# Feed-forward layers of a three-layer transformer block: split inputs tile by tile before the norm is known, apply the norm factor to the up projections' outputs

## The chip, the core and the metric

The kernel runs on one core of a Trainium2 chip. Its time is the device time of one execution in microseconds (us). Engines are called by these names: TensorE (PE, matrix products), VectorE (DVE), ScalarE (ACT), GpSimd (POOL), SyncE (SP, here only issuing loads).

## What is computed

Three layers over a sequence of 512 tokens of width 1024 in float32: a windowed-attention layer, a recurrent (RWKV) layer, and a layer that mixes three attentions. Each ends in a feed-forward part, and these three parts are what the change touches:

```
def rms_norm(x, g):
    y = xf * lax.rsqrt(jnp.mean(xf * xf, axis=-1, keepdims=True) + NORM_EPS)
    return (y * g.astype(F32)).astype(x.dtype)
...
        x = x + y
        x = x + conv_ffn(rms_norm(x, norm_ch[i]), ffn_w_up[i], ffn_conv_w[i], ffn_conv_b[i], ffn_w_down[i])
...
    u = h @ w_up                      # 1024 -> 5632
    acc = up[:, :s] * conv_w[0] + conv_b
    for t in range(1, CONV_WIDTH):    # three taps along the sequence
        acc = acc + up[:, t:t + s] * conv_w[t]
    gate, val = jnp.split(acc, 2, axis=-1)
    return (jax.nn.silu(gate) * val) @ w_down      # 2816 -> 1024
```

The third layer's feed-forward part has no convolution: silu(h @ w_gate) * (h @ w_up), then @ w_down. The factor rsqrt(mean(x*x)) is one number for each token, so it can be multiplied in before a product with weights or after it.

## The kernel before

**Layout.** Activations lie transposed: 128 features on the partitions, 512 tokens along the row. A matrix [128, 512] of this kind is one activation tile; x (`xT`) is 8 of them (`KT` = 8). A product with a weight matrix runs over output tiles (`tile()` on TensorE). The list `tile_table()` gives their order through the program: `swa_o` (8 tiles), `up0` (44), `down0` (8), the recurrent layer, `rw_o` (8), `up1` (44), `down1` (8), the third layer's attentions, `out` (8), `up2` (44), `down2` (8). An `up` tile sums over 8 input tiles kt, a `down` tile over 22.

**Split operands.** Each float32 operand is split into a high part and a low part (x minus high), and each kt costs three matmuls of 512 columns: high*high, low*high, high*low (lines 1503 to 1505), so an `up` tile is 24 matmuls. Weights come by SyncE into a ring of 5 pieces of up to 8 kt; ScalarE makes the high part (`split_high`, line 289), GpSimd the low part (`split_low`, line 298). The piece for the tile three ahead is split when a tile ends (`advance(t)`). Activations are split by ScalarE (`act_split`, line 499) and VectorE (`dve_split`, line 505); `wait_split` lets TensorE wait for the low part of one kt. `HS` holds the split inputs of the next product. In a float32 product that isn't split (the norm's sum, line 1585; the head sums, line 1538) one matmul instruction shows as two records.

**Output tiles** go to two PSUM banks in turn (`bank_of(t)`). Tile t may start when tile t-2's bank has been read for the last time; `release[t]` names the semaphore. For `swa_o`, `rw_o` and `out` it is the addition to x (`add_x`, line 2243 on VectorE).

**The norm ahead of a feed-forward part** (`ch0`, `ch1`, `ffn`). While the product before it streams, ScalarE squares each x tile after it was added (`square`, line 1850) and GpSimd sums the squares (line 2102). When the last one is in, TensorE multiplies by ones (`norm`, line 1585, into bank 7), ScalarE forms the factor by Ln and Exp (lines 1857 and 1858) in `M.nrs`, and VectorE multiplies x by gain and factor, tile by tile (line 2187), into `F.stmp`, from which the split is made. Only then can the first `up` tile's matmuls run, kt by kt.

**The up phase.** In layers 0 and 1 ScalarE reads the finished bank (line 1969: middle tap and bias, into `F.acc`), VectorE adds the outer taps from the same bank (lines 2372 and 2374), ScalarE takes Silu (line 1977), VectorE multiplies gate and value (line 2379) and the product is split into `F.hid`. In layer 2 ScalarE takes Silu from the bank (line 1988), and VectorE multiplies the other bank into it (line 2384). All engines run their own list of instructions in order; semaphores set the rest.

Of the kernel before, what the change touches and what calls it, by code (L numbers as in the profile page):

```python
# [15 lines left out]
P = 128  # L16
# [133 lines left out]
def build(nc, ctx, x_in, mem_in, w_in, vec_in, row_in, const_in, small_in, x_spill, out):  # L150
# [192 lines left out]
    M.score = at(o, NBUF, 512); o += NBUF * 512  # L343
    M.pts = at(o, 2, 512); o += 1024
# [5 lines left out]
    M.q = at(o, KT, T); o += KT * T  # L350
    M.k = at(o, 4, T); o += 4 * T
    M.v = at(o, TT, 256); o += TT * 256
    M.turned = at(o, 4, 512); o += 4 * 512
    kp_swa = at(o, CONST_SIZE[1]); o += CONST_SIZE[1]
# [6 lines left out]
    F.stmp = at(o, 2, 512); o += 1024  # L361
    assert o <= NORM, o
# [166 lines left out]
    o += 2 * KT * T  # L529
    R.r = at(o, KT, T); o += KT * T  # L530
# [44 lines left out]
    R.z = pair(CORE, 4, T) + pair(TMP, 2, T) + pair(TMP + 6 * 512, 2, T)  # L575
# [913 lines left out]
    def _(pe):  # L1489
# [21 lines left out]
        def fm(name, rhs, gate=None):  # L1511
            for k, t in enumerate(tiles_of[name]):
                tile(t, rhs, gate if k == 0 else None)
# [233 lines left out]
        fm("swa_o", h_split, gate=lambda kt: wait_split(pe, "swa_o", kt))  # L1747
        norm("ch0")
# [9 lines left out]
        norm("ch1")  # L1758
# [34 lines left out]
        norm("ffn")  # L1793
# [4 lines left out]
    def _(act):  # L1798
# [53 lines left out]
        def norm(name, width=T, dst=None, tmp=None, first=False):  # L1852
# [3 lines left out]
            r = M.nrs[:, 0:width]  # L1856
# [50 lines left out]
        def attend_swa():  # L1907
            for s in range(len(PAIRS) + 6):
# [21 lines left out]
                if 0 <= r < len(PAIRS) and r % TT == TT - 1:  # L1930
                    act.wait_ge(SW_O, r + 1)
                    act_split(act, "swa_o", r // TT, lambda p: OT_BANKS[r // TT % 2], HS[r // TT])
# [26 lines left out]
        def ffn(L):  # L1959
            if L < 2:  # L1960
                for n, t in enumerate(tiles_of[f"up{L}"]):
                    i, g = n // 2, n % 2
                    c = 44 * L + n
                    advance(t)
                    wait_tile(act, t)
# [620 lines left out]
```

## Time and profile before

| | us |
|---|---|
| median of 3 runs (3051.27 to 3064.58) | 3053.04 |
| the profiled execution | 3059.92 |
| its span in the trace | 3058.1 |

TensorE's granted clock is 0.976 of full speed on average. Durations below come from the profiled execution, whose span is 1.8 us shorter than its time. Rows of the timeline give start, busy time, engine, line, operation, output and inputs; in square brackets stands the time that the engine was idle before the row and what ended it. Rows that follow each other closely on one line are merged (x2). A row of groups gives count, busy us and mean ns. A matmul row overlaps the next: matmuls start 0.23 us apart at full clock although a row says 0.39.

### The profile page before, as it was taken

What the parts mean: (1) busy time and instruction counts of PE and PEld (TensorE: products, weight loads), DVE (VectorE), ACT (ScalarE), POOL (GpSimd) and SP (SyncE); (2) the same over time, 40 slices, a digit from 0 to 9 for tenths busy, and PEclk for the clock granted to TensorE, in tenths of its full rate; (3) what the DMA queues carried; (4) which work ended last, traced back from release to release, by engine and by line L of the source; (5) the groups of instructions that cost most, each with busy time, mean ns of one, the idle gap of its engine ahead of it and who ended that gap; (6) DMA issues with size and microseconds to landing.
All of it is one profiled execution on the core that took longest, in us unless ns stands there. A gap on an engine that the chain in (4) does not pass through costs nothing.

```text
span 3058.1 us, 55232 instructions
## 1 busy us (share of the span) xinstructions
PE 2852.6 (93%) x23558; PEld 2232.2 (73%) x23558; DVE 1122.0 (37%) x2425; ACT 1241.6 (41%) x2288; POOL 1153.5 (38%) x659
## 2 busy tenths in 40 slices
PE   6998999969999999988999989899999989999999
PEld 4666888847677777776888866477777777778887
DVE  3473333045656677653333111602211224321110
ACT  4473443223455555543443223534443444332221
POOL 3204444553443222213444444043333342534443
PEclk9999999979999999998999999899999999999999
DMA  3202332222210000011232222032211231323322
GB/s 135 62 8 76 96 97 92 94 77 81 86 45 7 7 7 7 5 36 56 90 97 94 92 89 66 4 122 74 80 62 65 72 101 47 107 76 97 96 89 78
DMA packets 59364, 211.96 MB, mean 69 GB/s; under 512 B 6833, under 2 KB 7089, under 8 KB 58737
## 3 DMA queue, kind: packets, MB, share of 16 engines
q1 hardware_dynamic: 56160, 192.96, 19.9%
q0 software_dynamic: 2384, 14.06, 1.3%
q8 instruction: 187, 3.06, 0.4%
q10 hardware_dynamic: 576, 1.41, 0.1%
q14 instruction: 57, 0.46, 0.1%
HBM read 204.21 MB, written 4.19 MB: 68 GB/s over the span
## 4 chain that ended last, share of the span: by engine, by line
PE 82%; DVE 9%; ACT 5%; issue 2%; POOL 1%; DMA 0%; POOLq 0%; SPq 0%; ACTq 0%; DVEq 0%
PE banks L1503 20%; PE banks L1505 20%; PE banks L1504 20%; PE banks L723 7%; DVE low L505 2%; PE banks L1624 2%; PE banks L1538 2%; PE banks L1602 1%; PE banks L638 1%; DVE arena L2187 1%; DVE arena L2215 1%; ACT arena L1827 1%; ACT arena L1826 1%; PE banks L774 1%; PE banks L716 1%
## 5 line engine op out<-in xcount | busy, mean ns | idle before, releaser
L298 POOL TENSOR_TENSOR low<-arena,high 128x1024 fp32r<-128x1024 f32 (+1 forms) x378 | 871.8, 2307 | 1408.0 <-ACT high L289 1407.9
L1503 PE MATMUL banks<-high,high 128*128 128x512 f32 (+1 forms) x2864 | 1168.5, 408 | 83.7 <-DVE low L505 65.2
L1504 PE MATMUL banks<-low,high 128*128 128x512 f32 (+1 forms) x2864 | 1131.7, 395 | 0.0
L1505 PE MATMUL banks<-high,low 128*128 128x512 f32 (+1 forms) x2864 | 1131.2, 395 | 0.0
L289 ACT ACTIVATE high<-arena 128x1024 fp32r<-128x1024 f32 (+1 forms) x378 | 383.8, 1016 | 938.3 <-PE banks L1505 931.5
L1503 PEld LDWEIGHTS banks<-high,high 128*128 128x128 f32 x2864 | 544.7, 190 | 263.6 <-issue 53.9
L1504 PEld LDWEIGHTS banks<-low,high 128*128 128x128 f32 x2864 | 546.0, 191 | 128.8 <-issue 12.3
L1505 PEld LDWEIGHTS banks<-high,low 128*128 128x128 f32 x2864 | 545.1, 190 | 125.4
L723 PE MATMUL banks<-arena 64*64 64x64 f32 x7680 | 291.5, 222 | 28.0 <-ACT arena L1018 12.2
L723 PEld LDWEIGHTS banks<-arena 64*64 64x64 f32 x7680 | 251.0, 135 | 86.9 <-ACT arena L1018 31.5
L1018 ACT ACTIVATE arena<-banks 128x256 f32<-128x256 f32 (+2 forms) x384 | 144.7, 384 | 173.5 <-PE banks L723 163.6
L2243 DVE TENSOR_TENSOR arena<-banks,arena 128x512 f32<-128x512 f32 x48 | 33.1, 692 | 449.8 <-PE banks L1505 442.7
L505 DVE TENSOR_TENSOR low<-arena,high 128x512 fp32r<-128x512 f32 (+1 forms) x182 | 166.2, 914 | 28.8 <-ACT high L499 27.5
L2372 DVE SCALAR_TENSOR_TENSOR arena<-banks,arena 128x511 f32<-128x511 f32 x88 | 66.0, 750 | 294.5 <-ACT arena L1969 294.5
L2215 DVE SCALAR_TENSOR_TENSOR arena<-banks,arena 128x512 f32<-128x512 f32 (+1 forms) x56 | 41.0, 732 | 328.1 <-ACT arena L1827 328.1
L499 ACT ACTIVATE high<-arena 128x512 fp32r<-128x512 f32 (+1 forms) x182 | 111.6, 615 | 95.3 <-DVE arena L1209 52.4
L1167 POOL TENSOR_TENSOR arena<-arena 128x128 f32<-128x128 f32 x64 | 27.7, 453 | 306.0 <-DVE arena L1426 305.9
L1400 DVE TENSOR_TENSOR arena<-banks,arena 128x128 f32<-128x128 f32 x320 | 88.3, 289 | 146.7 <-PE banks L723 144.5
L1826 ACT ACTIVATE arena<-banks,arena 128x512 f32<-128x512 f32 (+1 forms) x56 | 37.6, 672 | 163.2 <-PE banks L1538 163.2
L2384 DVE TENSOR_TENSOR arena<-banks,arena 128x512 f32<-128x512 f32 x22 | 15.2, 692 | 214.4 <-PE banks L1505 214.4
L1840 ACT ACTIVATE arena<-banks 128x512 f32<-128x512 f32 (+2 forms) x50 | 28.9, 579 | 145.6 <-PE banks L1505 145.5
L2374 DVE SCALAR_TENSOR_TENSOR arena<-banks,arena 128x511 f32<-128x511 f32 x88 | 66.0, 750 | 3.1
(222 smaller groups left out, 2711.5 us busy)
## 6 DMA issues: line engine op xcount, KB each, us to landing
arena<-weights SPq DMA_DIRECT2D x306, 512.0 KB, 3.5
arena<-weights SPq DMA_DIRECT2D x48, 448.0 KB, 3.2
arena<-weights SPq DMA_DIRECT2D x24, 256.0 KB, 2.6
arena<-tables POOLq DMA_DIRECT2D x13, 448.0 KB, 4.6
arena<-x_t SPq DMA_DIRECT2D x4, 512.0 KB, 7.3
x_spill<-arena POOLq DMA_DIRECT2D x1, 2048.0 KB, 9.1
arena<-small_weights POOLq DMA_DIRECT2D x16, 128.0 KB, 2.6
arena<-x_spill POOLq DMA_DIRECT2D x1, 2048.0 KB, 9.1
```

Source lines behind the costliest of these rows:

```text
L289: act.activation(wsplit[w % SPLITS][0][:, 0:n], ring[w % RING][:, 0:n], ACT.Copy).then_inc(w_high, 1)
L298: pool.tensor_tensor(lo[:, 0:n], ring[w % RING][:, 0:n], hi[:, 0:n].bitcast(F32), ALU.subtract).then_inc(w_low, 1)
L499: act.activation(dst[0], src((s0 + i) % 2), ACT.Copy).then_inc(act_high, 1)
L505: dve.tensor_tensor(dst[1], src((s0 + i) % 2), dst[0].bitcast(F32), ALU.subtract).then_inc(act_low, 1)
L723: mm = pe.matmul(bank[hf(p), col + C * q:col + C * q + C], lhs(hf(p), q), rhs(hf(p), q), start=True, stop=True)
L1018: a2.inc(act.activation(dst, PJ[h][:, 0:n], ACT.Copy), f"{name}_{h}")
L1400: d2.inc(dve.tensor_tensor(u, PI[h][:, 0:P], u, ALU.add), f"U{s}_{h}")
L1503: pe.matmul(dst, hi[:, c], x[0], start=kt == 0, stop=False)
L1504: pe.matmul(dst, hi[:, c], x[1], start=False, stop=False)
L1505: mm = pe.matmul(dst, lo[:, c], x[0], start=False, stop=kt == kts_of[t] - 1)
L1826: link(act.activation(r, psum[2 + H % 2][:, 0:width], ACT.Ln, bias=EPS, scale=1.0 / group))
L2215: dve.scalar_tensor_tensor(o_, bank[:, 0:width], gain, s.rs[:, H % 2, 0:width], ALU.mult, ALU.mult) \
```

## The change

The three norms before feed-forward parts (`ch0`, `ch1`, `ffn`) are no longer applied to x. `add_x` on VectorE multiplies each x tile by the gain alone as soon as it is added, into `F.stmp`, and both halves of the split are made while the product before is still streaming. TensorE runs the norm's sum as `mid` of the first `up` tile, behind its kt 4. The factor goes to a buffer of its own, `F.rs`. VectorE multiplies every `up` output tile by it into `F.up` (two buffers), which releases the bank (`up_scaled`); the middle tap, the outer taps, Silu and the gate's product read `F.up`, in SBUF, where they read PSUM before. VectorE's outer taps of tile n-1 now stand behind the scaling of tile n.

Since `HS` is now written while the product before is read, two inputs moved: the window attention's outputs are split into `M.o` instead of `HS`, with the layer's buffers laid out anew, and the recurrent layer's split outputs `R.z` lie in other places.

```diff
@@
+    M.o = pair(o, KT, T)
...
+    F.up = at(o, 2, 512); o += 1024
+    F.rs = at(o, 512); o += 512
...
-    for L in range(2):
+    up_scaled = sem("up_scaled")
+    for L in range(3):
         for n, t in enumerate(tiles_of[f"up{L}"]):
-            release[t] = (conv_done, 44 * L + n + 1)
-    for n, t in enumerate(tiles_of["up2"]):
-        release[t] = (hid_ready, 2 * FT + n // 2 + 1) if n % 2 else (glu_gate, n // 2 + 1)
+            release[t] = (up_scaled, 44 * L + n + 1)
...
-    R.z = pair(CORE, 4, T) + pair(TMP, 2, T) + pair(TMP + 6 * 512, 2, T)
+    R.z = [[nc.alloc_sbuf_tensor_at(f"z_{part}{j}", [P, T], F32R, offset=start + 4 * (a + j * T))[:, :]
+            for part, a in (("high", CORE), ("low", RAT))] for j in range(KT)]
@@ TensorE
         def ffn(L):
             name = ("ch0", "ch1", "ffn")[L]
-            fm(f"up{L}", h_split, gate=lambda kt: wait_split(pe, name, kt))
+            fm(f"up{L}", h_split, gate=lambda kt: wait_split(pe, name, kt), mid=lambda: norm(name))
...
-        norm("ch0")
         ffn(0)
@@ ScalarE
+            def square_and_split(j):
+                square(norm_name, j, xT)
+                if norm_name in ("ch0", "ch1", "ffn"):
+                    act_split(act, norm_name, j, lambda p: F.stmp[:, p, :], HS[j])
+
             for j, t in enumerate(tiles_of[name]):
                 if j and norm_name:
-                    square(norm_name, j - 1, xT)
+                    square_and_split(j - 1)
                 for p in pieces_of[t]:
                     if norm_name and p == pieces_of[tiles_of[name][-1]][-1]:
-                        square(norm_name, KT - 1, xT)
+                        square_and_split(KT - 1)
                     split_high(act, p + SPLITS)
...
         def ffn(L):
+            norm(("ch0", "ch1", "ffn")[L], to=F.rs)
+            for n, t in enumerate(tiles_of[f"up{L}"]):
+                i, g = n // 2, n % 2
+                c, m = 44 * L + n, FT * L + i
+                advance(t)
+                if L < 2:
+                    act.wait_ge(up_scaled, c + 1)
                     if c >= 4:
                         act.wait_ge(hid_ready, FT * L + i - 1)
                     col = L * 132 + 44 + g * FT + i
-                    act.activation(F.acc[:, c % 4, :], bank_of(t)[:, :], ACT.Identity,
+                    act.activation(F.acc[:, c % 4, :], F.up[:, n % 2, :], ACT.Identity,
...
-        norm("ch0", dst=HS, tmp=F.stmp)
         ffn(0)
@@ VectorE
-        def add_x(name):
+        def add_x(name, scaled=None):
+
+            def low(k):
+                dve_split(dve, scaled, k, lambda p: F.stmp[:, p, :], HS[k])
             for k, t in enumerate(tiles_of[name]):
                 wait_tile(dve, t)
                 dve.tensor_tensor(xT[:, k, :], bank_of(t)[:, :], xT[:, k, :], ALU.add).then_inc(x_ready, 1)
+                if scaled:
+                    g, o_ = NGAIN[scaled]
+                    dve.wait_ge(x_ready, XBASE[name] + k + 1)
+                    dve_free(dve, scaled, k)
+                    dve.tensor_scalar(F.stmp[:, (SG[scaled][0] + k) % 2, :], xT[:, k, :], vcol(g, o_ + k), None, ALU.mult) \
+                       .then_inc(N_H, 1)
+                    if k:
+                        low(k - 1)
+            if scaled:
+                low(KT - 1)
...
+            def taps(n):
+                g, i, c = n % 2, n // 2, 44 * L + n
+                a, b = F.acc[:, c % 4, :], F.up[:, g, :]
+                dve.wait_ge(sem("conv_mid"), c + 1)
+                link(dve.scalar_tensor_tensor(a[:, 1:T], b[:, 0:T - 1], vcol("conv_w", L * 132 + g * FT + i),
+                                              a[:, 1:T], ALU.mult, ALU.add))
+                dve.scalar_tensor_tensor(a[:, 0:T - 1], b[:, 1:T], vcol("conv_w", L * 132 + 88 + g * FT + i),
+                                         a[:, 0:T - 1], ALU.mult, ALU.add).then_inc(conv_done, 1)
...
+            dve.wait_ge(N_RS, NORMS.index(("ch0", "ch1", "ffn")[L]) + 1)
+            for n, t in enumerate(tiles):
+                wait_tile(dve, t)
+                if n >= 2 and L < 2:
+                    dve.wait_ge(conv_done, 44 * L + n - 1)
+                elif n >= 2:
+                    dve.wait_ge(*((hid_ready, 2 * FT + n // 2) if n % 2 else (glu_gate, n // 2)))
+                dve.tensor_tensor(F.up[:, n % 2, :], bank_of(t), F.rs, ALU.mult).then_inc(up_scaled, 1)
+                if L < 2:
+                    if n:
+                        taps(n - 1)
+                    if n >= 2 and n % 2 == 0:
+                        product(n // 2 - 1)
+                elif n % 2:
+                    product(n // 2)
...
-        add_x("swa_o")
-        norm("ch0", dst=HS, tmp=F.stmp)
+        add_x("swa_o", "ch0")
         ffn(0)
```

How the instruction lists move, by their order in the program. **VectorE, end of `swa_o` and start of `up0`.** Before, the eight additions stand together, then gain and factor (L2187) alternate with the low parts (L505) of `HS`:

```order
L2243 TENSOR_TENSOR arena<-banks,arena 128x512 x8
L2187 SCALAR_TENSOR_TENSOR arena<-arena 128x512 x2
L505 TENSOR_TENSOR low_57<-arena,high_56 128x512
L2187 SCALAR_TENSOR_TENSOR arena<-arena 128x512
L505 TENSOR_TENSOR low_59<-arena,high_58 128x512
```

Now the end of the same list reads (L2244 is the addition, L2249 the gain alone, L508 a low part, L2406 the scaling of an `up` output tile, L2380 and L2382 its outer taps):

```order
L2244 TENSOR_TENSOR arena<-banks,arena 128x512
L2249 TENSOR_SCALAR arena<-arena 128x512
L508 TENSOR_TENSOR low_69<-arena,high_68 128x512
L508 TENSOR_TENSOR low_71<-arena,high_70 128x512
L2406 TENSOR_TENSOR arena<-banks,arena 128x512 x2
L2380 SCALAR_TENSOR_TENSOR arena<-arena 128x511
L2382 SCALAR_TENSOR_TENSOR arena<-arena 128x511
```

All but the last addition's gain and low parts now stand between additions; behind the last one there are one gain and two low parts, where sixteen instructions stood.

**VectorE, one pair of tiles within `up0`.** Before (L2379 is the product of gate and value):

```order
L2372 SCALAR_TENSOR_TENSOR arena<-banks,arena 128x511
L2374 SCALAR_TENSOR_TENSOR arena<-banks,arena 128x511
L2372 SCALAR_TENSOR_TENSOR arena<-banks,arena 128x511
L2374 SCALAR_TENSOR_TENSOR arena<-banks,arena 128x511
L2379 TENSOR_TENSOR arena<-arena 128x512
L505 TENSOR_TENSOR low_75<-arena,high_74 128x512
```

Now (L2395 is the product):

```order
L2406 TENSOR_TENSOR arena<-banks,arena 128x512
L2380 SCALAR_TENSOR_TENSOR arena<-arena 128x511
L2382 SCALAR_TENSOR_TENSOR arena<-arena 128x511
L2406 TENSOR_TENSOR arena<-banks,arena 128x512
L2380 SCALAR_TENSOR_TENSOR arena<-arena 128x511
L2382 SCALAR_TENSOR_TENSOR arena<-arena 128x511
L2395 TENSOR_TENSOR arena<-arena 128x512
L508 TENSOR_TENSOR low_91<-arena,high_90 128x512
```

Two instructions with one input in PSUM are added to a pair, and the four taps lose their PSUM input: both their inputs are now in SBUF.

**TensorE, from `swa_o`'s last matmuls into `up0`.** Before, the norm's sum (L1585) stands between the two products:

```order
L1503 MATMUL banks<-high_70,high_50 128x512
L1504 MATMUL banks<-low_71,high_50 128x512
L1505 MATMUL banks<-high_70,low_51 128x512
L1585 MATMUL banks<-arena 128x512
L1503 MATMUL banks<-high_56,high_52 128x512
```

Now it (L1590) stands behind 15 of `up0`'s first 24 matmuls (kt 4 ends there, kt 5 follows):

```order
L1508 MATMUL banks<-high_64,high_52 128x512
L1509 MATMUL banks<-low_65,high_52 128x512
L1510 MATMUL banks<-high_64,low_53 128x512
L1590 MATMUL banks<-arena 128x512
L1508 MATMUL banks<-high_66,high_52 128x512
```

## Rows read from the trace of the kernel before

**Rows 1.** The page: busy us (share of the span) and instructions of each engine.
```profile
PE 2852.6 (93%) x23558; PEld 2232.2 (73%) x23558; DVE 1122.0 (37%) x2425; ACT 1241.6 (41%) x2288; POOL 1153.5 (38%) x659
```

**Rows 2.** Stretches: length, busy us (instructions) by engine, clock, DMA share, GB/s.
```profile
270.00:279.00 9.00, 7.73 (x25) 4.53 (x24) 7.57 (x12) 3.36 (x7) 0.00 (x0) 0.85 0.00 0
300.00:400.00 100.00, 100.00 (x432) 81.05 (x431) 38.95 (x54) 40.43 (x54) 43.37 (x18) 1.00 0.30 95
...
1436.00:1450.00 14.00, 9.15 (x20) 4.59 (x20) 10.14 (x15) 6.31 (x10) 2.54 (x2) 0.63 0.12 39
```

**Rows 3.** VectorE's timeline at the norm ahead of `up0`.
```profile
261.19 0.69 DVE L2243 TENSOR_TENSOR arena<-banks,arena 128x512 f32<-128x512 f32 x1 [4.89 <-PE banks L1505]
266.58 0.75 DVE L2187 SCALAR_TENSOR_TENSOR arena<-arena 128x512 f32<-128x512 f32 x1 [4.70 <-ACT arena L1858]
```

**Rows 4.** TensorE's timeline at the same place.
```profile
263.94 1.13 PE L1585 MATMUL banks<-arena 128*128 128x512 f32 x2 [2.79 <-POOL arena L2102]
268.87 0.77 PE L1503 MATMUL banks<-high,high 128*128 128x512 f32 x1 [3.80 <-DVE low L505]
...
274.33 0.51 PE L1503 MATMUL banks<-high,high 128*128 128x512 f32 x1 [0.42 <-DVE low L505]
...
275.72 0.50 PE L1503 MATMUL banks<-high,high 128*128 128x512 f32 x1 [0.42 <-DVE low L505]
```

**Rows 5.** ScalarE's timeline: the ends of `up0`'s first and second tile.
```profile
278.96 1.06 ACT L289 ACTIVATE high<-arena 128x1024 fp32r<-128x1024 f32 x1 [1.85 <-PE banks L1505]
...
284.54 1.06 ACT L289 ACTIVATE high<-arena 128x1024 fp32r<-128x1024 f32 x1 [3.85 <-PE banks L1505]
```

**Rows 6.** VectorE and ScalarE around the norm ahead of `up1`.
```profile
1433.55 0.69 DVE L2243 TENSOR_TENSOR arena<-banks,arena 128x512 f32<-128x512 f32 x1 [4.89 <-PE banks L1505]
1451.99 1.06 ACT L289 ACTIVATE high<-arena 128x1024 fp32r<-128x1024 f32 x1 [1.85 <-PE banks L1505]
```

**Rows 7.** The same two around the norm ahead of `up2`.
```profile
2674.78 0.69 DVE L2243 TENSOR_TENSOR arena<-banks,arena 128x512 f32<-128x512 f32 x1 [4.87 <-PE banks L1505]
2692.53 1.06 ACT L289 ACTIVATE high<-arena 128x1024 fp32r<-128x1024 f32 x1 [1.84 <-PE banks L1505]
```

**Rows 8.** TensorE: an unsplit 128x512 product between split matmuls, clock up.
```profile
42.16 0.40 PE L1505 MATMUL banks<-high,low 128*128 128x512 f32 x1
42.40 1.02 PE L1538 MATMUL banks<-arena 128*128 128x512 f32 x2
...
43.48 0.39 PE L1504 MATMUL banks<-low,high 128*128 128x512 f32 x1
```

**Rows 9.** ScalarE's last square, GpSimd's last sum, and Exp ahead of `up0`.
```profile
261.92 0.63 ACT L1850 ACTIVATE arena<-arena 128x512 f32<-128x512 f32 x1 [4.67 <-DVE arena L2243]
...
262.62 1.27 POOL L2102 TENSOR_TENSOR arena<-arena 128x512 f32<-128x512 f32 x1 [2.17 <-ACT arena L1850]
...
265.83 0.72 ACT L1858 ACTIVATE arena<-arena 128x512 f32<-128x512 f32 x1
```

**Rows 10.** VectorE, one line in the window attention: ns min/median/max, forms.
```profile
L2318 DVE TENSOR_SCALAR arena<-arena x64: 345/382/423, 139.5 to 213.0; 128x256 f32<-128x256 f32 x32, 128x384 f32<-128x384 f32 x32
```

**Rows 11.** Groups by line in 280 to 520 (`up0`): busy us, mean ns, idle before.
```profile
L2372 DVE SCALAR_TENSOR_TENSOR arena<-banks,arena 128x511 f32<-128x511 f32 x43 | 32.2, 750 | 143.3 <-ACT arena L1969 143.3
L2379 DVE TENSOR_TENSOR arena<-arena 128x512 f32<-128x512 f32 x21 | 16.1, 766 | 1.2 <-ACT arena L1977 0.5
L505 DVE TENSOR_TENSOR low<-arena,high 128x512 fp32r<-128x512 f32 x20 | 13.6, 679 | 0.0
L298 POOL TENSOR_TENSOR low<-arena,high 128x1024 fp32r<-128x1024 f32 x42 | 101.2, 2409 | 143.8 <-ACT high L289 143.8
```

**Rows 12.** GpSimd and VectorE at the end of `mix2`; then the latter's line, ns min/median/max.
```profile
2630.96 2.49 POOL L298 TENSOR_TENSOR low<-arena,high 128x1024 fp32r<-128x1024 f32 x1 [0.40 <-ACT high L289]
2631.21 3.39 DVE L505 TENSOR_TENSOR low<-arena,high 128x512 fp32r<-128x512 f32 x2
L505 DVE TENSOR_TENSOR low<-arena,high x2: 678/1734/2789, 2631.2 to 2633.9; 128x512 fp32r<-128x512 f32 x2
```

More of the change, by code:

```diff
@@ L529, in build @@
     o += 2 * KT * T
+    RAT = o
     R.r = at(o, KT, T); o += KT * T
@@ L1746, in _ @@
         attend_swa()
-        fm("swa_o", h_split, gate=lambda kt: wait_split(pe, "swa_o", kt))
-        norm("ch0")
+        fm("swa_o", lambda kt: M.o[kt], gate=lambda kt: wait_split(pe, "swa_o", kt))
         ffn(0)
@@ L1850, in square, with norm @@
             act.activation(M.nsq[:, i % 2, 0:width], src[:, j, :], ACT.Square).then_inc(N_SQ, 1)
-        def norm(name, width=T, dst=None, tmp=None, first=False):
+        def norm(name, width=T, dst=None, tmp=None, first=False, to=M.nrs):
             n = NORMS.index(name)
             act.wait_ge(N_ST, n + 1)
-            r = M.nrs[:, 0:width]
+            r = to[:, 0:width]
             link(act.activation(r, psum[7][:, 0:width], ACT.Ln, bias=EPS, scale=1.0 / D))
@@ L1977, in ffn @@
                         act.activation(F.sg[:, m % 2, :], F.acc[:, (44 * L + 2 * i) % 4, :], ACT.Silu).then_inc(sem("silu"), 1)
[L1978 to L1990 removed]
+                elif g == 0:
+                    act.wait_ge(up_scaled, c + 1)
+                    if i >= 2:
+                        act.wait_ge(hid_ready, m - 1)
+                    act.activation(F.sg[:, i % 2, :], F.up[:, 0, :], ACT.Silu).then_inc(glu_gate, 1)
+                if g and i:
+                    act_split(act, f"hid{L}", i - 1, lambda p: F.stmp[:, p, :], F.hid[i - 1])
             act_split(act, f"hid{L}", FT - 1, lambda p: F.stmp[:, p, :], F.hid[FT - 1])
@@ L2016, in _ @@
         stream_tiles("rw_o", "ch1")
-        norm("ch1", dst=HS, tmp=F.stmp)
         ffn(1)
@@ L2081, in _ @@
         stream_tiles("out", "ffn")
-        norm("ffn", dst=HS, tmp=F.stmp)
         ffn(2)
@@ L2363, in ffn @@
             tiles = tiles_of[f"up{L}"]
-            for i in range(FT):
-                tmp = F.stmp[:, (SG[f"hid{L}"][0] + i) % 2, :]
+            def taps(n):
[6 more added lines that the diff above has]
+                                         a[:, 0:T - 1], ALU.mult, ALU.add).then_inc(conv_done, 1)
@@ L2366, in ffn, with product @@
+            def product(i):
                 dve_free(dve, f"hid{L}", i)
                 if L < 2:
-                    for g in range(2):
-                        n = 44 * L + 2 * i + g
-                        a, b = F.acc[:, n % 4, :], bank_of(tiles[2 * i + g])
-                        dve.wait_ge(sem("conv_mid"), n + 1)
-                        link(dve.scalar_tensor_tensor(a[:, 1:T], b[:, 0:T - 1], vcol("conv_w", L * 132 + g * FT + i),
-                                                      a[:, 1:T], ALU.mult, ALU.add))
-                        dve.scalar_tensor_tensor(a[:, 0:T - 1], b[:, 1:T], vcol("conv_w", L * 132 + 88 + g * FT + i),
-                                                 a[:, 0:T - 1], ALU.mult, ALU.add).then_inc(conv_done, 1)
@@ L2388, in ffn @@
+            if L < 2:
+                taps(2 * FT - 1)
+                product(FT - 1)
             low(FT - 1)
@@ L2415, in _ @@
         dve.wait_ge(x_back, 16)
-        add_x("rw_o")
-        norm("ch1", dst=HS, tmp=F.stmp)
+        add_x("rw_o", "ch1")
         ffn(1)
@@ L2473, in _ @@
         mix(2)
-        add_x("out")
-        norm("ffn", dst=HS, tmp=F.stmp)
+        add_x("out", "ffn")
         ffn(2)
```

53 lines of the change are left out of this document (15 added, 38 removed).

## Prediction

> **What bounds the kernel now.** I read the page's busy times first. TensorE is busy for 2852.6 of 3058.1 us, 93%, and no other engine for more than 41% [rows 1], so only time in which TensorE stands still or runs slowly can be won. The table of stretches shows where it does neither: from 300 to 400, inside `up0`, it is busy for all 100.00 us at clock 1.00 [rows 2]. An `up` tile there takes 284.54 - 278.96 = 5.58 us from end to end [rows 5], 0.2325 us a matmul. The timelines then show the place that the change is about. VectorE begins the last addition of `swa_o` at 261.19, right at that tile's end; the first matmul of `up0` starts at 268.87 [rows 3, 4], and the first tile's end shows as the weight split that ScalarE starts at 278.96 [rows 5]. The reader is to see two losses in these 17.77 us: the wait for sum, factor and first split, and then a tile that is fed with one kt every 275.72 - 274.33 = 1.39 us [rows 4], where three matmuls take 0.70. The clock is low on top: 0.85 from 270 to 279, and 0.63 from 1436 to 1450 at the second norm [rows 2]. The same distance is 1451.99 - 1433.55 = 18.44 us ahead of `up1` [rows 6] and 2692.53 - 2674.78 = 17.75 us ahead of `up2` [rows 7].
>
> **What the change takes from these distances.** If TensorE goes straight on, the distance from the last addition's start to the first `up` tile's end is one tile, 5.58 us; both marks start within hundredths of a us behind a tile's end, which I neglect. To this comes the norm's sum, which now stands in the tile. Its price in the flow is in [rows 8]: from the matmul at 42.16 to the one at 43.48 there are 1.32 us with one split matmul and one unsplit product between them; without the latter it would be two steps of 0.23, so it costs 0.86. After the change the distance is 5.58 + 0.86 = 6.44 us, and the gains are 17.77 - 6.44 = 11.33, 18.44 - 6.44 = 12.00 and 17.75 - 6.44 = 11.31. The sum is 34.6 us.
>
> **Is everything there in time?** Let E be the end of the last tile of `swa_o`. Its addition takes 0.69 [rows 3], to E+0.75. The gain alone on 128x512 has no row; the same operation on 256 and 384 columns takes 0.345 to 0.423 [rows 10], and a 512-column instruction with two SBUF inputs 0.75 [rows 3], so it lies between 0.4 and 0.75 and I take 0.5, nearer to the row of its own form. Low parts of kt 0 to 5 were made between earlier additions, where VectorE sat idle for 4.89 us at each tile [rows 3]. Low part of kt 6 ends near E+2.0. For kt 7 ScalarE must square first (0.63 from 261.92, about E+0.8 [rows 9]), then make the high part at about E+1.5 to 2.1; GpSimd's last sum, 1.27 [rows 9], may come ahead of the low part, which then ends near E+4.1. TensorE reaches kt 6 at E+4.2 + 0.86 and kt 7 at E+4.9 + 0.86. Both are in time, kt 7 with 1.6 us to spare. The norm's sum comes behind 15 matmuls, E+3.5. Before, it started at 263.94 [rows 4], 2.8 us behind an E of 261.1; if GpSimd is held up by one low part (0.68) it is E+3.5, so a wait of 0 to 0.5 is possible here. I take none. The factor was ready when Exp ended, 265.83 + 0.72 - 263.94 = 2.6 us behind the sum's start [rows 4, 9]; that gives E+6.1, and the first `up` tile ends at E+6.44, so VectorE can scale it at once.
>
> **Costs in the up phase.** VectorE gets one 128x512 multiplication per `up` tile, 132 in all. The nearest row is the addition of the same shape with one PSUM input, 0.69 us [rows 3]. For a pair of tiles of `up0` VectorE had four taps of 0.75, one product of 0.77 and one low part of 0.68 [rows 11], 4.45 us of 2 x 5.58 = 11.16; now it has 4.45 + 1.38 = 5.83. The bank of tile n is free at about 0.8 us behind its end, while tile n+2 starts one tile, 5.58 us, later. Price: nothing, hidden by TensorE's own 5.58. ScalarE waits for the scaling before its middle tap; behind that wait in its list are Silu, one high part and the next tile's weight split. That piece is wanted by TensorE only two tiles, 11.16 us, after the tile's end that starts it, and split plus GpSimd's low part take 1.06 + 2.41 = 3.5 [rows 5, 11]. At the end of `up0` the last hidden tile is now late by about a scaling, a pair of taps and a GpSimd instruction, at most 0.7 + 1.5 + 2.4 more; it is wanted by the first `down` tile behind 21 kt, 21 x 0.70 = 14.6 us. Nothing there either. The added multiplications and gains are thus free as long as VectorE keeps up. `M.o` and `R.z` only move data; they cost nothing where neither adds an instruction. The window attention's and recurrent layer's last splits keep their place in the lists.
>
> **What speaks against it: VectorE and GpSimd get in each other's way.** [rows 12] show a low part, two SBUF inputs, that began at 2631.21 beside a GpSimd split begun at 2630.96 for 2.49 us: it lasted 2.789 instead of 0.678 and ended at 2634.0, which is GpSimd's end, 2633.45, and most of a low part. The taps with a PSUM input ran at 0.750 on average next to 2.41 us of GpSimd work in every tile [rows 11]. The change turns these four taps of a pair into instructions with two SBUF inputs. So add what excludes each other: 4 x 0.75 + 0.77 + 0.68 + 2 x 2.41 = 9.27 us of 11.16 for a pair, and with the two scalings, if none overlaps GpSimd, 10.65. It still fits, by 0.5 us in the strictest count and 1.9 in the other; lateness doesn't pile up, since a scaling that comes late runs beside GpSimd. I take nothing, with 0 to 1 us a pair as bounds.
>
> The Trainium skill says the same as a rule (page "SBUF — State Buffer", section "SBUF: two separate sides"): a VectorE instruction with two SBUF inputs and a GpSimd instruction hold the shared ports exclusively, and the other one waits for the whole instruction. [rows 12] agree, 2.789 against 0.678 us. The rule is what rival C rests on. By it as by the row the sum stays at 34.6 us, since 10.65 is under 11.16; without either, VectorE alone would need 5.83.
>
> **The rivals.**
> A, the forecast: TensorE goes straight on at all three places, -34.6 us. Chance 0.72.
> B, gaps remain: the sum or the last split comes late by the port exclusion or by GpSimd's queue (its last sum stands behind the sum before it), 1 to 3 us at each of three norms, or the factor delays the first banks. Gain 34.6 - 3 to 34.6 - 9, that is 25.6 to 31.6 us. For it speaks the 0 to 0.5 us that I found as slack for the sum; against it that each late item has two tiles' cover. Chance 0.18.
> C, the other side: exclusion on the shared ports makes VectorE the bound of `up0` and `up1`. It decides when what excludes each other and the scalings take more than 11.16 us a pair; each further us costs 44 us over 44 pairs, so the kernel is slower than before from 11.16 + 34.6 / 44 = 11.95 us on, against my 10.65. At 12.2 us it would be 1.04 x 44 - 34.6 = +11 us. Chance 0.04.
> D, the gain isn't there: the 11 us come back elsewhere, say as low clock later or a late weight ring, and the time stays within 10 us. Against it: the stretch from 300 to 400 shows clock 1.00 under full load [rows 2]. Chance 0.06.
>
> **The numbers.** The profiled execution took 3059.92 us, 6.9 above the median of the runs, 3053.04. By the profile the change gives 3059.92 - 34.6 = 3025.3; a gain in waits doesn't depend on which run it is taken from, so for the median I predict 3053.04 - 34.6 = 3018.4 us. The runs of before spread from 3051 to 3065, so a median can be off by some 5 us either way. The range reaches from 3018.4 - 9 = 3009.4 (the spread of runs, and a few us that a rounded duration may hide) to 3053 - 22 = 3031, which takes in case B with some spread. About 0.5% (15 us) is what a measurement of this kernel can tell from no change. Faster by more than that, under 3037.8, are A, B and a little of D: 0.91. Within it: most of D and an edge of C, 0.06. Slower: 0.03.
>
> **What the next profile would show.** Right: between the last addition of `swa_o`, `rw_o` or `out` and the first weight split of the `up` phase 6.4 us instead of 17.8 to 18.4; no TensorE row with an idle time over 0.5 us there; clock 1.00 throughout; tiles of `up0` still 5.58 us apart; VectorE's taps longer than 0.75 on average, because one in a tile waits for GpSimd. Wrong would be: `up` tiles over 5.6 us apart (C), a TensorE wait at the norm's sum or at kt 6 and 7 (B), a stretch of low clock or of waits that before wasn't there (D). The time before the last `swa_o` tile and the `down` phases should be the same to within 1 us.

## The result and the profile after

The changed kernel takes 3024.27 us (median of 4 runs, 3016.72 to 3026.67) beside 3053.37 us for the kernel before (4 runs). The ratio is 0.9893 with an interval of 0.9863 to 0.9924, which is 32.7 us less, with 23 to 42 us as bounds; the ratio is estimated from all the runs, while the two medians alone differ by 29.1 us, inside these bounds. Run again beside 17 runs of the kernel before (`changed_again` below) the ratio is 0.9893 again, now with 0.9879 to 0.9908. The forecast was 34.6 us less, and 3018.4 us.

The page of the changed kernel, in the form of [rows 1]:

```profile
span 3024.9 us, 55470 instructions
...
PE 2841.6 (94%) x23558; PEld 2230.9 (74%) x23558; DVE 1415.7 (47%) x2557; ACT 1248.3 (41%) x2288; POOL 1170.0 (39%) x659
```

The span fell from 3058.1 to 3024.9, by 33.2 us. TensorE runs the same 23558 instructions. VectorE has 132 instructions more, one for each `up` tile, and 293.7 us more of busy time, far more than 132 x 0.69 = 91 us. The rest is not work; below it turns out to be mostly waiting.

VectorE's timeline at the end of `swa_o`, which answers to [rows 3]:

```profile
260.64 0.69 DVE L2244 TENSOR_TENSOR arena<-banks,arena 128x512 f32<-128x512 f32 x1 [3.76 <-PE banks L1510]
261.37 0.49 DVE L2249 TENSOR_SCALAR arena<-arena 128x512 f32<-128x512 f32 x1
261.77 2.39 DVE L508 TENSOR_TENSOR low<-arena,high 128x512 fp32r<-128x512 f32 x2
267.15 0.69 DVE L2406 TENSOR_TENSOR arena<-banks,arena 128x512 f32<-128x512 f32 x1 [2.98 <-PE banks L1510]
```

ScalarE's, which answers to [rows 5, 9]:

```profile
261.37 0.64 ACT L1852 ACTIVATE arena<-arena 128x512 f32<-128x512 f32 x1 [4.14 <-DVE arena L2244]
261.91 0.61 ACT L502 ACTIVATE high<-arena 128x512 fp32r<-128x512 f32 x1
...
265.71 0.72 ACT L1860 ACTIVATE arena<-arena 128x512 f32<-128x512 f32 x1
267.14 1.06 ACT L289 ACTIVATE high<-arena 128x1024 fp32r<-128x1024 f32 x1 [0.70 <-PE banks L1510]
...
272.71 1.06 ACT L289 ACTIVATE high<-arena 128x1024 fp32r<-128x1024 f32 x1 [3.81 <-PE banks L1510]
```

TensorE's, which answers to [rows 4, 8]:

```profile
263.70 0.40 PE L1510 MATMUL banks<-high,low 128*128 128x512 f32 x1
263.93 1.02 PE L1590 MATMUL banks<-arena 128*128 128x512 f32 x2
264.39 0.80 PE L1508 MATMUL banks<-high,high 128*128 128x512 f32 x1
265.02 0.39 PE L1509 MATMUL banks<-low,high 128*128 128x512 f32 x1
```

From the last addition (260.64) to the first `up` tile's end (267.14) there are now 6.50 us where there were 17.77. No TensorE row there has an idle time in square brackets, and the sum lies in the flow: from the start of the matmul at 263.70 to the start of the one at 265.02 there are 1.32 us, which is two steps of 0.23 for the matmuls at 263.70 and 264.39 and 0.86 for the sum between them. Low parts end at 264.16, the factor at 266.43, and VectorE scales the first bank at once, at 267.15. The other two places, VectorE's last addition and then ScalarE's split at the first tile's end:

```profile
1423.83 0.69 DVE L2244 TENSOR_TENSOR arena<-banks,arena 128x512 f32<-128x512 f32 x1 [3.79 <-PE banks L1510]
1430.33 1.06 ACT L289 ACTIVATE high<-arena 128x1024 fp32r<-128x1024 f32 x1 [0.70 <-PE banks L1510]
2652.80 0.69 DVE L2244 TENSOR_TENSOR arena<-banks,arena 128x512 f32<-128x512 f32 x1 [3.76 <-PE banks L1510]
2659.29 1.06 ACT L289 ACTIVATE high<-arena 128x1024 fp32r<-128x1024 f32 x1 [0.70 <-PE banks L1510]
```

The distances are 6.50 and 6.49 us, where [rows 6] gave 18.44 and [rows 7] 17.75. The three gains are 11.27 + 11.94 + 11.26 = 34.47 us. Stretches around the places and in the up phases, with the columns of [rows 2]:

```profile
225.00:275.00 50.00, 50.00 (x215) 40.21 (x214) 17.06 (x26) 20.17 (x28) 33.41 (x18) 1.00 0.30 95
270.00:390.00 120.00, 120.00 (x518) 97.30 (x517) 97.22 (x83) 50.70 (x65) 51.94 (x22) 1.00 0.29 95
1390.00:1430.00 40.00, 40.00 (x170) 31.92 (x171) 19.29 (x23) 17.52 (x26) 32.31 (x16) 1.00 0.29 93
1430.00:1660.00 230.00, 230.00 (x992) 186.46 (x991) 192.08 (x162) 97.24 (x124) 99.01 (x41) 1.00 0.30 96
```

TensorE is busy all the time at clock 1.00, also in the stretch that answers to 1436 to 1450 before, where the clock was 0.63. At the third place, from 2650 to 2690, the clock is 1.00 too. In `up0`, groups of VectorE from 270 to 510 (against [rows 11]):

```profile
L2382 DVE SCALAR_TENSOR_TENSOR arena<-arena 128x511 f32<-128x511 f32 x43 | 114.8, 2670 | 1.5
L2380 DVE SCALAR_TENSOR_TENSOR arena<-arena 128x511 f32<-128x511 f32 x43 | 31.9, 742 | 0.0
L2406 DVE TENSOR_TENSOR arena<-banks,arena 128x512 f32<-128x512 f32 x43 | 29.7, 692 | 38.0 <-PE banks L1510 37.5
```

One tap in a tile takes 2670 ns instead of 750, the other 742 (the forecast had said that one in a tile would wait for GpSimd). The timeline of one tile says why, VectorE first, then GpSimd:

```profile
401.53 0.74 DVE L2380 SCALAR_TENSOR_TENSOR arena<-arena 128x511 f32<-128x511 f32 x1
402.31 2.77 DVE L2382 SCALAR_TENSOR_TENSOR arena<-arena 128x511 f32<-128x511 f32 x1
405.17 0.69 DVE L2395 TENSOR_TENSOR arena<-arena 128x512 f32<-128x512 f32 x1
```

```profile
402.12 2.41 POOL L298 TENSOR_TENSOR low<-arena,high 128x1024 fp32r<-128x1024 f32 x1 [3.15 <-ACT high L289]
```

GpSimd's split began at 402.12 and ended at 404.53. The tap that came 0.19 us later ended at 405.08, 0.55 behind it, which is most of its own 0.75. Over 88 tiles with taps this comes to 88 x 1.92 = 169 us, the larger part of the 293.7.

The Trainium skill (page "SBUF — State Buffer", section "SBUF: two separate sides") has the rule that the later of the two waits for the whole instruction of the earlier. The trace agrees: the tap begun beside GpSimd's split took 2.77 us where the one before it took 0.74.

### The profile page after: what moved, and what is told of

The parts are those of the page before. It is cut to its first block, busy times and chain, and to the rows that moved or that the text cites. A ratio compares the mean times of both kernels' runs of the same rounds, so it can differ in the third digit from the quotient of the medians.

```text
span 3024.9 us, 55470 instructions
## 1 busy us (share of the span) xinstructions
PE 2841.6 (94%) x23558; PEld 2230.9 (74%) x23558; DVE 1415.7 (47%) x2557; ACT 1248.3 (41%) x2288; POOL 1170.0 (39%) x659
## 4 chain that ended last, share of the span: by engine, by line
PE 83%; DVE 8%; ACT 5%; issue 2%; POOL 1%; DMA 1%; POOLq 0%; SPq 0%; ACTq 0%; DVEq 0%
PE banks L1508 21%; PE banks L1509 20%; PE banks L1510 20%; PE banks L728 7%; PE banks L1629 2%; PE banks L1543 2%; DVE low L508 2%; PE banks L1607 1%; PE banks L643 1%; DVE arena L2213 1%; ACT arena L1829 1%; ACT arena L1828 1%; PE banks L779 1%; PE banks L721 1%; DVE arena L1214 1%
## 5 line engine op out<-in xcount | busy, mean ns | idle before, releaser
L298 POOL TENSOR_TENSOR low<-arena,high 128x1024 fp32r<-128x1024 f32 (+1 forms) x378 | 886.9, 2347 | 1358.2 <-ACT high L289 1358.1
L1508 PE MATMUL banks<-high,high 128*128 128x512 f32 (+1 forms) x2816 | 1145.5, 407 | 69.3 <-DVE low L508 50.9
L1509 PE MATMUL banks<-low,high 128*128 128x512 f32 (+1 forms) x2816 | 1110.1, 394 | 0.0
L1510 PE MATMUL banks<-high,low 128*128 128x512 f32 (+1 forms) x2816 | 1110.0, 394 | 0.0
L1509 PEld LDWEIGHTS banks<-low,high 128*128 128x128 f32 x2816 | 535.3, 190 | 127.9 <-issue 13.0
L1510 PEld LDWEIGHTS banks<-high,low 128*128 128x128 f32 x2816 | 534.4, 190 | 122.9
L2382 DVE SCALAR_TENSOR_TENSOR arena<-arena 128x511 f32<-128x511 f32 x88 | 235.2, 2672 | 3.1
L2244 DVE TENSOR_TENSOR arena<-banks,arena 128x512 f32<-128x512 f32 x48 | 33.2, 691 | 419.5 <-PE banks L1510 411.1
L508 DVE TENSOR_TENSOR low<-arena,high 128x512 fp32r<-128x512 f32 (+1 forms) x174 | 205.8, 1184 | 26.9 <-ACT high L502 25.6
L2406 DVE TENSOR_TENSOR arena<-banks,arena 128x512 f32<-128x512 f32 x132 | 91.3, 692 | 219.6 <-PE banks L1510 218.4
L2232 DVE COPY arena<-banks 128x512 f32<-128x512 f32 (+1 forms) x30 | 19.7, 656 | 109.7 <-PE banks L1563 109.7
```

What stands on the lines that cost most here:

```text
L298: pool.tensor_tensor(lo[:, 0:n], ring[w % RING][:, 0:n], hi[:, 0:n].bitcast(F32), ALU.subtract).then_inc(w_low, 1)
L508: dve.tensor_tensor(dst[1], src((s0 + i) % 2), dst[0].bitcast(F32), ALU.subtract).then_inc(act_low, 1)
L1508: pe.matmul(dst, hi[:, c], x[0], start=kt == 0, stop=False)
L1509: pe.matmul(dst, hi[:, c], x[1], start=False, stop=False)
L1510: mm = pe.matmul(dst, lo[:, c], x[0], start=False, stop=kt == kts_of[t] - 1)
L2382: dve.scalar_tensor_tensor(a[:, 0:T - 1], b[:, 1:T], vcol("conv_w", L * 132 + 88 + g * FT + i), a[:, 0:T - 1], ALU.mult, ALU.add).then_inc ...
```

## The experiments

Ratios are to the kernel before in the same job (medians 3059.09, 3058.49 and 3058.13 us). Distance is the time from the last addition's start to the first `up` tile's end; 6.50 in the changed kernel.

**1. The moved buffers alone.** `layout_only` is the kernel before with the new buffers `M.o` and `R.z`.

```diff
+    M.o = pair(o, KT, T)
...
+    R.z = [[nc.alloc_sbuf_tensor_at(...
...
-            fm("swa_o", h_split, ...
+            fm("swa_o", lambda kt: M.o[kt], ...
```

> Kernel before, with only the two moves of buffers (the window attention's outputs into M.o, R.z in its new places). Theory (buffers are free, the gain is the three norm gaps): same time as before, within 3 us, the three distances from last addition to first up tile's end still 17.8, 18.4 and 17.8 us. Rival (the moved buffers cost the 2 us that the recurrent part was longer in the changed kernel's profile): about 2 us slower, with the low clock at the end of the recurrent part always 16 instead of 10.5 us long.

Measured: 3057.64 us, ratio 1.0000 (0.9989 to 1.0011). The move costs nothing that can be measured, and nothing of the gain is in it.

**2. Layers apart.** `third_only` changes layer 2 alone, `first_two` layers 0 and 1, `changed_again` is the changed kernel beside `first_two`. The lines are from `first_two`; its other edits are left out.

```diff
-            fm(f"up{L}", h_split, gate=..., mid=lambda: norm(name))
+            if L == 2:
+                norm(name)
+            fm(f"up{L}", h_split, gate=..., mid=(lambda: norm(name)) if L < 2 else None)
```

> Changed kernel, but layers 0 and 1 have their feed-forward parts as before (factor on x, taps from PSUM); only layer 2 is changed. Theory (three gaps, each worth its own 11.3 to 12 us, nothing lost in the up phases): 11.3 us faster than before, and 23 us slower than the changed kernel. Rival (the taps that now exclude GpSimd cost layers 0 and 1 part of their gain): much nearer to the changed kernel's time than that, or faster than it.

> Layers 0 and 1 as in the changed kernel, layer 2 as before. If the gain is three separate places whose distances from last addition to first up tile add up: 11.3 + 12.0 = 23.3 us off the kernel before, ratio about 0.9924, and the third place's distance stays at 17.7 us. If a part of the gain belongs to the feed-forward stages as a whole or to the recurrent part (rival), it is not 23: below 20 or above 27.

> The changed kernel once more, beside first_two and paired_first and in more rounds. Theory: 34.5 us less than before (the three distances 11.27 + 11.94 + 11.26), ratio 0.9887. Rival: 30 us or less, if the three distances overstate the gain by what the later tiles lose; 38 or more if the recurrent part shares in it.

Measured: `third_only` 3047.12 us, 0.9954 (0.9940 to 0.9969), which is 14.1 less with 9.5 to 18.4 as bounds; `first_two` 3033.59, 0.9929 (0.9916 to 0.9943), 21.7 less (17.4 to 25.7); `changed_again` 3024.52, 32.7 less by the ratio (28.1 to 37.0), 33.6 by the medians. In the traces the changed places stand at 6.49 to 6.51 us each, and `first_two`'s third, unchanged, at 17.77. By these distances the parts are 11.3 and 23.2 us, inside the bounds of both kernels. Here are `third_only`'s last addition and first tile's end, 6.49 apart:

```profile
2664.04 0.69 DVE L2255 TENSOR_TENSOR arena<-banks,arena 128x512 f32<-128x512 f32 x1 [3.76 <-PE banks L1512]
...
2670.53 1.06 ACT L289 ACTIVATE high<-arena 128x1024 fp32r<-128x1024 f32 x1 [0.70 <-PE banks L1512]
```

The gain is three separate places that add up.

**3. The two halves of the idea.** `splits_late` keeps the factor on the output tiles but multiplies by the gain and splits only behind the last addition, as before; ScalarE's high parts move there too (not shown below). It shows what taking the factor off the inputs is worth without the early split.

```diff
-                if scaled:
+            if scaled:
+                for k in range(KT):
                     ...
                     dve.tensor_scalar(F.stmp..., xT[:, k, :], vcol(g, o_ + k), None, ALU.mult)
```

> Changed kernel, but gain and both split halves of all eight x tiles come after the last addition, in one go; the factor stays deferred to the outputs. Theory (the gap was made of the wait for the factor, some 5.3 us, and of a feed at 1.2 to 1.4 us a kt instead of 0.7 us, and the two add up): the distance becomes 3.4 us to the first low part, 7 x 1.2 us of feed and one kt, about 12.5 us instead of 17.8 before and 6.5 in the changed kernel, so 16 us faster than before. Rival (deferring the factor is what counts, the split is hidden anyway): 34 us faster, like the changed kernel. Rival (streaming the split is what counts): no faster than before by more than 5 us.

Measured: 3040.96 us, 0.9939 (0.9928 to 0.9951), 18.7 less. TensorE behind the last `swa_o` tile (the addition starts at 262.06):

```profile
265.46 0.47 PE L1508 MATMUL banks<-high,high 128*128 128x512 f32 x1 [3.43 <-DVE low L508]
...
266.56 0.52 PE L1508 MATMUL banks<-high,high 128*128 128x512 f32 x1 [0.17 <-DVE low L508]
```

VectorE's low parts of kt 1 and 2 there:

```profile
265.82 0.68 DVE L508 TENSOR_TENSOR low<-arena,high 128x512 fp32r<-128x512 f32 x1
...
267.01 0.69 DVE L508 TENSOR_TENSOR low<-arena,high 128x512 fp32r<-128x512 f32 x1
```

The first matmul comes 3.40 us behind the addition's start instead of 7.68 ([rows 3, 4]: 268.87 - 261.19), and the split of one more kt is then made every 1.2 us, with the clock at 0.66 on average from 265.4 to 270.4. ScalarE marks only the second tile's end, at 17.92, 17.89 and 17.90 us behind the last additions; before, this was 23.35, 24.01 and 23.33, and in the changed kernel 12.07 or 12.08 at all three. So 17.0 of the 34.5 us are the factor off the path, and the other half is the split while the product before streams. The second half can't be had alone: x can only be split before the factor is known if the factor goes elsewhere.

**4. Where the sum stands.** The changed kernel runs it behind kt 4. `sum_early` runs it behind kt 0, `sum_late` behind kt 7. In the lines below `mid` is the sum, and `tile`'s last argument, `at_kt`, is the kt behind which it runs.

```diff
-                    if mid and kt == kts_of[t] // 2:
+                    if mid and kt == (kts_of[t] // 2 if at_kt is None else at_kt):
...
-                tile(t, rhs, None if k else gate, None if k else mid)
+                tile(t, rhs, None if k else gate, None if k else mid, 0)    # sum_late: 7
```

> Changed kernel with the norm's sum behind the first kt of the first up tile instead of the fifth. Theory (GpSimd's last sum is in 3.0 us behind the tile's end and the fifth kt ends at 3.5, so the place has 0.3 to 0.5 us of slack): TensorE waits 3.0 - 0.7 = 2.3 us there, three times, 7 us slower than the changed kernel (27 us faster than before). Rival (the sum isn't near the path, the slack is large): no wait, time as the changed kernel.

> Changed kernel with the norm's sum behind the last kt of the first up tile. Theory: TensorE doesn't wait for it in either place, the factor comes 2.1 us later than the fifth kt allows, at about 8.2 us behind the last product's end, the first scaling is late by 1.7 us and the bank it frees isn't wanted before 12 us: same time as the changed kernel within 2 us, first scaling later in the trace. Rival (the factor's lateness passes on to TensorE through the banks): 5 us slower.

Measured: `sum_early` 3034.60 us, 0.9924 (0.9909 to 0.9938); `sum_late` 3026.95, 0.9893 (0.9878 to 0.9908). With the sum early, TensorE waits for GpSimd's last sum of squares at each place, 2.33 to 2.34 us, here at the first two:

```profile
264.59 1.12 PE L1590 MATMUL banks<-arena 128*128 128x512 f32 x2 [2.34 <-POOL arena L2100]
1425.38 1.13 PE L1590 MATMUL banks<-arena 128*128 128x512 f32 x2 [2.33 <-POOL arena L2100]
```

The distances are 10.65, 10.65 and 10.71 us, so a wait of 2.33 costs 4.15 to 4.21. `sum_early`'s clock around it:

```profile
264.50:266.50 2.00, 1.91 (x5) 1.25 (x6) 0.58 (x1) 0.72 (x2) 2.00 (x2) 0.84 0.00 0
266.50:269.50 3.00, 3.00 (x9) 2.31 (x8) 0.00 (x0) 0.69 (x1) 0.82 (x1) 0.54 0.38 91
269.50:272.50 3.00, 3.00 (x15) 2.41 (x14) 0.24 (x1) 0.25 (x1) 0.00 (x0) 1.00 0.22 89
```

The clock falls behind the wait and is back at 269.5 (9 matmuls in the second stretch, 15 in the third). What it takes away is 2.00 x 0.16 + 3.00 x 0.46 = 1.7 us, nearly all of the other 1.8. The expectation counted the wait alone, and 7 us for three places was too little: the trace gives 12.5, and the ratios of the two kernels are 0.0031 apart, 9.5 us, with bounds of some 6 us either way, which take in both figures.

`sum_late` makes the factor late for the first tile:

```profile
268.29 0.69 DVE L2406 TENSOR_TENSOR arena<-banks,arena 128x512 f32<-128x512 f32 x1 [4.42 <-ACT arena L1860]
```

Nothing follows from it, since the third tile only wants that bank at the end of the second, which comes 12.09 us behind the last addition, 12.07 in the changed kernel.

**5. How much VectorE can take.** The changed kernel with extra multiplications in `up0` and `up1` whose results nobody uses: one or two for each tile with two SBUF inputs (`extra_sbuf1`, `extra_sbuf2`), or two with one input in PSUM (`extra_psum2`).

```diff
                 dve.tensor_tensor(F.up[:, n % 2, :], bank_of(t), F.rs, ALU.mult).then_inc(up_scaled, 1)
+                for e in range(2 if L < 2 else 0):
+                    ...
+                    dve.tensor_tensor(psum[2 + e], F.rs, xT[:, e, :], ALU.mult).then_inc(sem("extra"), 1)
+                    # extra_psum2: psum[2 + e] <- bank_of(t), F.rs, ahead of the scaling
```

> Changed kernel with one more VectorE multiplication for each up tile of layers 0 and 1, two SBUF inputs, result unused. Theory (what excludes each other counts, 9.27 + 2 x 0.69 = 10.65 of 11.15 us a pair, scalings with a PSUM input run beside GpSimd): no slower than the changed kernel, tiles still 5.58 us apart. Rival (everything on VectorE and GpSimd adds up, 10.65 + 1.38 = 12.03 us a pair): 0.9 us a pair, 38 us slower than the changed kernel.

> The same with two more such multiplications for each up tile. Theory: 9.27 + 4 x 0.69 = 12.03 us a pair is over 11.15, VectorE becomes the bound of up0 and up1: 0.9 us a pair over 44 pairs, 38 us slower than the changed kernel, about as slow as before. Rival (VectorE's own work is all that counts, 5.83 + 2.76 = 8.6 us a pair, GpSimd yields): no slower. Rival (everything adds up, 13.4 us a pair): 99 us slower.

> Changed kernel with two more VectorE multiplications for each up tile of layers 0 and 1, one input in PSUM, ahead of the scaling. VectorE has the same added time as with two added multiplications of SBUF inputs. Theory (only instructions with two SBUF inputs exclude GpSimd): what excludes each other stays 9.27 us a pair and VectorE's own work is 8.6, so no slower than the changed kernel by more than 5 us. Rival (all VectorE work adds to GpSimd's, 13.4 us a pair): 99 us slower; rival (the count is of VectorE's time alone): no slower, and no slower with SBUF inputs either.

Measured: 3026.66 us, 0.9894 (0.9877 to 0.9911); 3060.37, 1.0007 (0.9996 to 1.0019); 3027.24, 0.9887 (0.9868 to 0.9907). One extra multiplication with two SBUF inputs is free, the second costs the whole gain, 34 us over 44 pairs or 0.8 a pair, where 0.9 was expected. The rival for the first, that the scalings count too (12.03 us a pair), is out. In `extra_sbuf2`, from 310 to 520, a group of TensorE and VectorE's scalings:

```profile
L1508 PE MATMUL banks<-high,high 128*128 128x512 f32 x278 | 111.5, 401 | 12.2 <-DVE arena L2406 12.2
```

```profile
L2411 DVE TENSOR_TENSOR banks<-arena 128x512 f32<-128x512 f32 x70 | 45.1, 688 | 0.0
...
L2406 DVE TENSOR_TENSOR arena<-banks,arena 128x512 f32<-128x512 f32 x35 | 24.0, 684 | 1.8
```

35 scalings in 210 us are 12.0 us a pair, and TensorE waits for them. The same stretch of `extra_psum2`:

```profile
L2410 DVE TENSOR_TENSOR banks<-banks,arena 128x512 f32<-128x512 f32 x72 | 46.5, 692 | 11.4 <-PE banks L1510 11.4
```

It runs as many extra instructions of the same length, 692 against 688 ns. VectorE still has idle time left (11.4 us before these), TensorE waits for nothing and the kernel keeps its gain. The extra instructions also stand in another place of the list, ahead of the scaling and not behind it. The trace of `extra_psum2` says that the place is not the reason: here two of them lie beside a split of GpSimd, and neither they nor the split (2.40 us) are longer for it.

```profile
407.64 1.29 DVE L2410 TENSOR_TENSOR banks<-banks,arena 128x512 f32<-128x512 f32 x2
407.80 2.40 POOL L298 TENSOR_TENSOR low<-arena,high 128x1024 fp32r<-128x1024 f32 x1 [2.80 <-ACT high L289]
```

So it is not VectorE's work that is the limit, but its work that excludes GpSimd's.

**6. Another way to fill the wait.** `paired_first` is the kernel before, with the first two `up` tiles multiplied alternately, one kt of each.

```diff
-            fm(f"up{L}", h_split, gate=lambda kt: wait_split(pe, name, kt))
+            two_tiles(tiles_of[f"up{L}"][0], h_split, lambda kt: wait_split(pe, name, kt))
+            for t in tiles_of[f"up{L}"][2:]:
+                tile(t, h_split)
```

> The kernel before, with the input split after normalising as it was, but the first two up tiles of each of the three places multiplied alternately, one k tile of each at a time, so that TensorE has 6 matmuls (about 1.39 us) for each split of 1.39 us instead of 3. Theory: the wait for splits is then filled by the second tile's work, the second tile ends when the first did, and a place gains one tile's matmuls, about 5.6 us: 17 us in all, ratio about 0.9945. Rivals: no gain, if the first tile's wait stays whole and the second's work only moves (ratio 1.000); or 34 us, if the pairing alone hides all that the change hides (0.989).

Measured: 3066.03 us (12 runs), ratio 1.0027 (1.0015 to 1.0040), 8 us more and not 17 less. The theory was too hopeful already for the second tile, and what was won there was lost at the third. TensorE at the start of `up0` and at the third tile, then the tap of VectorE that the third tile waits for:

```profile
269.54 0.76 PE L1527 MATMUL banks<-high,high 128*128 128x512 f32 x1 [3.80 <-DVE low L505]
...
282.25 0.40 PE L1529 MATMUL banks<-high,low 128*128 128x512 f32 x1
285.46 0.50 PE L1503 MATMUL banks<-high,high 128*128 128x512 f32 x1 [2.82 <-DVE arena L2376]
...
284.66 0.75 DVE L2376 SCALAR_TENSOR_TENSOR arena<-banks,arena 128x511 f32<-128x511 f32 x1
```

The pair is done 20.19 us behind the last addition (282.05 - 261.86), where the second tile was done after 284.54 - 261.19 = 23.35 before. That is 3.16 us won, not 5.6 (2.57 and 2.98 at the other places): the first matmul still comes 7.68 us behind the addition, and 48 matmuls take 11.16 us even at full clock, so the end could not come before 18.84; the clock, 0.51 from 269.4 to 273.4, made up the rest. And now both banks come full together. The third tile needs the first of them, and only from then on do ScalarE (a weight split, then the middle tap) and VectorE (two taps) read it, until 285.41. The third tile waits 2.82 us, where before these readings lay beside the second tile's matmuls. Then the clock is low again:

```profile
282.00:285.40 3.40, 0.65 (x3) 0.19 (x1) 1.49 (x2) 3.34 (x4) 2.22 (x1) 1.00 0.00 0
285.40:291.00 5.60, 5.54 (x17) 4.42 (x18) 2.51 (x4) 1.91 (x2) 2.48 (x2) 0.70 0.58 181
```

The third tile ends 31.09 us behind the last addition, 28.93 before; at the other places 30.82 against 29.59 and 29.31 against 28.91. That is 3.8 us lost. The other 4 us of the median are not found in the one profiled execution, whose span is 3058.4 (3058.1 before); they stay open.

## Why the prediction was right

**The distance of 6.44 us.** It measured 6.50, 6.50 and 6.49. One tile of 5.58 and a sum of 0.86 were the right terms, the sum measured 0.86 in its new place too, and the 34.6 us of the sum came out as 34.47. `first_two` and `third_only` show that the places add up, `splits_late` that each of the two steps is worth about half, and `layout_only` that the moved buffers are worth nothing. Rival A, confirmed. The runs alone are coarser than this: their 32.7 us less, with 28 to 37 as bounds, fit the sum and would fit 3 us less as well; the distances in the traces decide.

**The absolute time, 3018.4 against 3024.27.** This was off by 5.9 us, and not by the mechanism. The step is "for the median I predict 3053.04 - 34.6": the median of three runs was low. In the three later jobs 13 to 17 runs of the kernel before gave 3058.13 to 3059.09; with the last job's, 3058.13 - 34.6 = 3023.5, against 3024.52 for the changed kernel beside them. The text had allowed 5 us either way for it.

**Is everything there in time?** The gain alone, taken at 0.5 us, takes 0.49. The last low part, foreseen at E+4.1, ended at 264.16, E+3.6 with E = 260.6; it began beside GpSimd's last sum and ended 0.55 behind its end. GpSimd's last sum started at 262.08 and took 1.53, so the sum was ready at E+3.0, while TensorE came for it at E+3.3: no wait, with 0.3 us in hand. The prediction allowed a wait of 0 to 0.5 here and took none, because it had the sum held up by a whole low part (0.68); it was held up by 0.26, so the choice was right by a small margin and not by its own reckoning. This is the tightest place of the change; `sum_early` shows what stands behind it, and `sum_late` that one could put the sum three kt later at no price. Rival B's gaps are not in any trace of the changed kernel.

**VectorE's count.** The forecast named rows of 9.27 us a pair that exclude each other and 10.65 with the scalings. Measured, VectorE's own rows from 270 to 510 are 206.7 us for 21.5 pairs, 9.6 a pair with the waits in them, and 1.9 us a pair idle, most of it waiting for TensorE. Against 10.65 this is 1 us less: a tap waits 1.92 us and not GpSimd's whole 2.41, since in the tile shown GpSimd's split began 0.15 us before the first tap's end and the second tap ended 0.55 and not 0.75 behind the split. Rival C's price was good: with tiles 12.0 us a pair apart, in `extra_sbuf2`, the kernel takes as long as before, against 11.95 in the prediction. But rival C set this price against the count with the scalings, and that count is the wrong one: `extra_sbuf1` has 10.65 + 1.38 = 12.03 us by it and is as fast as the changed kernel, `extra_sbuf2` has 13.4. The count without them, 9.27, 10.65 and 12.03 us a pair in the three kernels, fits all three. So the margin was 1.9 us a pair and not 0.5.

**Low clock and rival D.** The clock is 1.00 at all three places. What stood at 0.85 and 0.63 in [rows 2] is gone with the waits and is part of the gain.

**"The time before the last tile and the down phases should be the same."** The recurrent layer is not the same: from the last addition of `down0` to the first of `rw_o` there are 759.59 us, where there were 757.62. With the 0.7 us that other stretches gave, this is why the span fell by 33.2 and not 34.47. It is not the change's: the same distance is 752.83 in `layout_only`, 752.98 in `extra_sbuf1`, 752.97 in `extra_psum2`, 759.17 in `sum_late` and 760.28 in `changed_again`. The clock at its end, in the changed kernel and in `extra_psum2`:

```profile
1366.00:1376.00 10.00, 10.00 (x30) 3.74 (x28) 5.41 (x9) 1.42 (x5) 0.00 (x0) 0.50 0.00 0
1376.00:1389.20 13.20, 13.20 (x52) 10.71 (x51) 2.76 (x5) 3.14 (x5) 0.00 (x0) 0.83 0.00 0
```

```profile
1359.00:1370.00 11.00, 8.23 (x109) 4.32 (x108) 6.29 (x15) 2.52 (x10) 0.00 (x0) 1.00 0.01 1
1370.00:1382.70 12.70, 11.26 (x51) 9.24 (x52) 4.17 (x8) 3.42 (x6) 0.00 (x0) 1.00 0.00 0
```

The last matmuls of the recurrent layer meet either level of the clock. Over the last 50 us of it the clock is 0.83 in the changed kernel and in `changed_again`, 0.86 in `sum_late`, 0.97 in `layout_only` and `extra_sbuf1`, and 1.00 in `extra_psum2`. Why one execution meets the lower one and another doesn't was not tried.

## What to carry to other kernels

A norm's factor that is one number for each token can be moved behind the product, and then two things come off the path: the factor itself, and the split that had to wait for it. Each was worth about half here, and what they leave is one tile and the sum, 6.50 us where 6.44 were reckoned.
Before work is moved to VectorE beside a busy GpSimd, count by inputs: instructions with two SBUF inputs plus GpSimd's own time are one budget, instructions with a PSUM input stand outside it. By this count the kernel ran free at 9.27 and at 10.65 us of 11.16 and lost all its gain at 12.03.
A few us of waiting before a matmul-bound stretch cost more than they look, since here the clock fell behind them (4.15 us for a wait of 2.33); a tile order that fills one wait may only carry it to the place where both banks come free.

## What the hardware showed that was not expected

- A wait of 2.33 us on TensorE cost 4.15 us, the clock at 0.54 over the 3 us that began 1.9 us behind the wait's end.
- GpSimd gives way too: its weight split took 2.88 us at 256.27 where a low part of VectorE, begun at 256.20, ran beside it, against 2.41 in the tile shown above, and 2781 ns on average in `extra_sbuf2` against 2404 in `extra_psum2`.
- The recurrent layer, untouched, takes 751.5 to 760.3 us from one execution to the next: the five traces above 757 us have a clock of 0.83 to 0.90 over its last 50 us, the seven below 754 have 0.97 to 1.00, and `paired_first` lies between, 755.4 at 0.86. A gain below 9 us can't be read from one pair of spans; it has to be read from distances at the place itself.
